# Seven block products for eight from the third feature tile on in the first feed-forward of a two-block model kernel

## What is computed

```python
u = rmsnorm(h, ffn_pre_norm[i])
gate, up = jnp.split(u @ w_gate_up[i], [D_FF], axis=-1)
y = (jax.nn.silu(gate) * up) @ w_down[i]
h = h + rmsnorm(y, ffn_post_norm[i])
```

## Time and profile before

| what | us |
|---|---|
| median of 3 runs | 2981.14 (2980.92 to 2981.69) |
| the profiled execution | 2984.09 |
| its span, first to last instruction | 2982.8 |
| TensorE busy | 2856.0 (96%) |
| VectorE busy | 1855.8 (62%) |
| ScalarE busy | 1205.5 (40%) |
| mean granted TensorE clock | 0.975 of full speed |

### The profile page before, as it was taken

How to read it: one execution, slowest core, us unless ns; L and a number is a source line. 1 busy time by engine, 2 the same in 40 slices (tenths; PEclk the granted TensorE clock), 3 DMA queues, 4 the chain that set the end, 5 groups by cost and what they waited for, 6 DMA issues and landing times.

```text
span 2982.8 us, 36065 instructions
## 1 busy us (share of the span) xinstructions
PE 2856.0 (96%) x14312; PEld 2390.3 (80%) x14312; DVE 1855.8 (62%) x2615; ACT 1205.5 (40%) x1810; POOL 71.3 (2%) x44
## 2 busy tenths in 40 slices
PE   8999989999999999999999977899999999999998
PEld 6878878887788888888778856788887888888887
DVE  4147668625766666667641277577457777777774
ACT  3144446634433323333331166776433333333432
POOL 0002210010000000000000000000000000000000
PEclk9999999999999999999999989887999999999999
DMA  4111130032211111113122100000211111111122
GB/s 170 50 32 46 57 118 19 2 126 78 106 52 50 55 57 50 50 57 127 50 85 64 36 15 10 22 1 1 93 42 43 50 57 57 50 50 57 57 92 85
DMA packets 47831, 172.99 MB, mean 58 GB/s; under 512 B 5648, under 2 KB 6160, under 8 KB 47664
## 3 DMA queue, kind: packets, MB, share of 16 engines
q1 hardware_dynamic: 47664, 170.68, 17.1%
HBM read 145.23 MB, written 25.43 MB: 57 GB/s over the span
## 4 chain that ended last, share of the span: by engine, by line
PE 86%; DVE 8%; ACT 3%; issue 2%; DMA 0%; SPq 0%; DVEq 0%; ACTq 0%
PE PS L295 14%; PE PS L297 14%; PE PS L299 13%; PE PS L1596 8%; PE PS L1597 8%; PE PS L1598 8%; PE PS L483 2%; PE PS L485 2%; PE PS L484 2%; PE PS L1184 2%; PE PS L706 2%; PE PS L3116 1%; PE PS L1154 1%; PE PS L1169 1%; DVE H L2788 1%
## 5 line engine op out<-in xcount | busy, mean ns | idle before, releaser
L1596 PE MATMUL PS<-u_hi_f,w_hi 128*128 128x512 f32 x624 | 242.7, 389 | 0.0
L1597 PE MATMUL PS<-u_lo_f,w_hi 128*128 128x512 f32 x624 | 242.7, 389 | 0.0
L1598 PE MATMUL PS<-u_hi_f,w_lo 128*128 128x512 f32 x624 | 242.7, 389 | 0.0
L289 DVE TENSOR_TENSOR w_lo<-w_raw,w_hi 128x1024 fp32r<-128x1024 f32 x93 | 116.1, 1252 | 202.3 <-ACT w_hi L283 202.3
L1545 ACT ACTIVATE w_hi<-weight_sums 128x512 fp32r<-128x512 f32 x156 | 98.1, 629 | 355.9 <-DVE weight_sums L1566 197.1
L283 ACT ACTIVATE w_hi<-w_raw 128x1024 fp32r<-128x1024 f32 x93 | 97.7, 1055 | 282.2 <-PE PS L299 143.2
L295 PE MATMUL PS<-f_ah,w_hi 128*128 128x512 f32 x640 | 197.1, 389 | 0.1
L297 PE MATMUL PS<-f_al,w_hi 128*128 128x512 f32 x640 | 197.0, 389 | 0.0
L299 PE MATMUL PS<-f_ah,w_lo 128*128 128x512 f32 x640 | 197.0, 389 | 0.0
L1551 DVE TENSOR_TENSOR w_lo<-w_raw,w_hi 128x512 fp32r<-128x512 f32 x205 | 137.2, 687 | 93.0 <-ACT w_hi L1545 93.0
L1596 PE MATMUL PS<-f_T_hi,w_hi 128*128 128x512 f32 x468 | 182.8, 391 | 1.9 <-issue 1.9
(11 more groups left out here) (447 smaller groups left out, 6572.5 us busy)
## 6 DMA issues: line engine op xcount, KB each, us to landing
w_raw<-in_weights SPq DMA_DIRECT2D x215, 512.0 KB, 3.5
H<-in_x_t SPq DMA_DIRECT2D x16, 512.0 KB, 4.2
h_kept<-H SPq DMA_DIRECT2D x16, 512.0 KB, 5.1
H<-h_kept SPq DMA_DIRECT2D x16, 512.0 KB, 6.8
stick_kept<-stick_stage SPq DMA_DIRECT2D x12, 512.0 KB, 2.9
mixer<-stick_kept SPq DMA_DIRECT2D x9, 512.0 KB, 7.2
p_kept<-p_stage SPq DMA_DIRECT2D x8, 512.0 KB, 3.9
p_pp<-p_kept SPq DMA_DIRECT2D x8, 512.0 KB, 8.1
```

The source lines that it names most:

```text
L289: dve.tensor_tensor(self.w_lo[i][:], self.w_raw[i][:], self.w_hi[i][:].bitcast(F32), ALU.subtract).then_inc(*self.s("w_lo").up(g))
L1596: pe.matmul(out, hi[:, self.chunk(k)], rh, start=opens and k == 0, stop=False, skip_group_check=True)
L1597: pe.matmul(out, hi[:, self.chunk(k)], rl, start=False, stop=False, skip_group_check=True)
L1598: mm = pe.matmul(out, lo[:, self.chunk(k)], rh, start=False, stop=k == 3, skip_group_check=True)
```

## The change

FAST_FROM of the first feed-forward goes from 3 to 2 and its skips go. The order of the operand parts on ScalarE and VectorE is rewritten around it: the half-width blocks 0 and 1 (A11, S1) stand before the copy of the rows, blocks 2 and 3 after tile 0; VectorE makes S1 and S2 before the raw operands; T2's low parts follow T1's in tile 0, and T3's stand between tile 1's gate and up. The whole splits of gates[2] and ups[2] are gone.

```diff
--- before.py
+++ after.py
@@ -39,8 +39,8 @@
 WINO = [("A11", "B11", 0), ("S1", "T1", 1), ("S2", "T2", 0), ("A12", "B21", 2), ("S3", "T3", 0), ("S4", "B22", 1),
         ("A22", "T4", 0)]
 WINO_BANKS = [(0, 1, 2), (3, 4, 6)]
-FAST_FROM = (3, 2)
-FAST_SKIPS = ((5, 9, 13), ())
+FAST_FROM = (2, 2)
+FAST_SKIPS = ((), ())
 AHEAD = 4
 
 FILL_HEAD, FILL, FILL_TAIL = 2, [3, 3, 3, 2, 2, 2, 1], [2, 1, 1, 2]
@@ -2043,14 +2043,10 @@
         self.act_statistics_root(tag)
         if n:
             self.act_split(gates[0] + RING)
-        if n:
-            for m in range(2):
-                self.act_ff_block(n, m)
+        for m in range(2):
+            self.act_ff_block(n, m)
         self.act_statistics_rows(tag, self.f_rows[n][:])
         for t in range(FAST_FROM[n]):
-            if n == 0 and t == 2:
-                for m in range(2):
-                    self.act_ff_block(n, m)
             act.wait_ge(*self.dve_freed(self.ff_pairs(t)[0], tag, "gate", t))
             if n == 1:
                 w, at = self.gains, self.gains_at["conv"][0] + 4 * t
@@ -2063,12 +2059,10 @@
             if t == 0:
                 self.act_ff_ah0(n)
             if n == 0 and t == 0:
-                self.act_split(gates[2])
                 self.act_ff_highs(n, ("T2", "T3"))
-            elif n == 0 and t == 1:
-                self.act_split(ups[2])
+            if n == 0 and t == 1:
                 self.act_ff_ah(n, 1)
-            elif t == 0:
+            if t == 0:
                 for m in range(2, 4):
                     self.act_ff_block(n, m)
         self.act_ff_fast(n)
@@ -2107,14 +2101,12 @@
         self.dve_statistics(tag, rows[:])
         if n:
             self.dve_split(gates[0] + RING)
-        if n == 0:
-            for k in range(4):
-                self.dve_ff_raw_operands(n, k)
-        else:
-            for m in range(4):
-                self.dve_ff_sum(n, m)
-            for m in range(2):
-                self.dve_ff_block(n, m)
+        for m in range(4):
+            self.dve_ff_sum(n, m)
+        for m in range(2):
+            self.dve_ff_block(n, m)
+        for k in range(4 if n == 0 else 0):
+            self.dve_ff_raw_operands(n, k)
         dve.wait_ge(*self.act_freed(3, tag, "rows"))
         for t in range(FAST_FROM[n]):
             pg, pu = self.ff_pairs(t)
@@ -2131,10 +2123,8 @@
                     dve.wait_ge(*self.s("f_gated").at(n, t - 1))
                 dve.tensor_tensor(sg[:], self.pair(pg), rows[:], ALU.mult).then_inc(*self.dve_frees(pg, tag, "gate", t))
             if n == 0 and t == 1:
-                self.dve_split(ups[2])
-            if n == 0 and t == 2:
-                for m in range(2):
-                    self.dve_ff_block(n, m)
+                for k in range(4):
+                    self.dve_ff_low(n, "T3", k)
             dve.wait_ge(*self.s("w_used").at(ups[t]))
             if n == 0 and t:
                 dve.wait_ge(*self.s("f_al").at(n, t - 1))
@@ -2145,14 +2135,13 @@
             if n == 0 and t == 0:
                 for i in range(5, KT):
                     dve.wait_ge(*self.d(f"p2_stored{i % 3}").at(i))
-            if n == 0:
-                for k in range(4):
-                    self.dve_ff_low(n, ("T1", "T3", "T2")[t], k)
+            if n == 0 and t == 0:
+                for x in ("T1", "T2"):
+                    for k in range(4):
+                        self.dve_ff_low(n, x, k)
             if t == 0 or n == 0 and t == 1:
                 self.dve_ff_al(n, t)
-            if n == 0 and t == 0:
-                self.dve_split(gates[2])
-            elif t == 0:
+            if t == 0:
                 for m in range(2, 4):
                     self.dve_ff_block(n, m)
                 self.dve_ff_sum(n, 4)
```

## The result

The median went from 2981.14 us to **2989.41 us** (7 runs, 2987.65 to 2992.63): a ratio of 1.0032, with a 95% interval of 1.0023 to 1.0041. 2990.5 us was predicted, in a range of 2987.5 to 2994. The kernel before, run 7 times beside it, spread from 2974.66 to 2983.31 us. The span of the profiled execution went from 2982.8 to 2988.0 us.

What follows compares the result with a forecast made beforehand. TensorE's own stream, 86% of the chain, was taken as the bound, so a later down step passes on whole. 0.5 - 2.7 - 4.6 + 14.2 + 2.0 = +9.4 us, taking the median from 2981.14 to 2990.5 us, range 2987.5 to 2994.

Steps and rivals of the forecast that it cites:

- The path into the wait: Tile 2's head: ups[1] product starts about 766.6 us, raw operands 4.0 us later, second block finished at 783.0 us.
- The rows copy 0.5 us later: ScalarE's copy of the statistics' rows, now behind S1's block, delays TensorE's ups[1] product: 0.5 us more.
- The wait: Before tile 2's third block product, S2 x T2, TensorE waits for ScalarE's copy of the first bank: 14.2 us more.
- The clock: After the new wait in tile 2, TensorE's matmuls run at a lower clock: 2.0 us more.
- What goes: Before tile 2, the old gates[2] split wait and its low clock go, 4.6 us less; fewer matmuls, 2.7 us less.
- The twelve matmuls: Tile 2 goes from 96 to 84 matmuls, twelve fewer at 0.227 us each: 2.7 us less.
- The down step's start: Down projection of tiles 0 and 1 in the first feed-forward begins at 812.8 us, not 803.4.
- Moved loads and skips at nothing: Later loads of units 45 and 46 and the dropped half-buffer skips in the first feed-forward cost nothing.
- B: Wait before tile 2's third block only as small as in the second feed-forward: -3.2 us, 2977.9 us; chance 0.06.
- C: Shorter third-block wait, T2's low parts and copy ready by some 790 us: +2 to +5 us; chance 0.04.
- D: A second wait behind the first, from late VectorE work or unit 45: 3 to 6 us more; chance 0.08.
- Rival A: First bank's copy done by 783 us, so no third-block wait: -6.8 us, 2974.3 us; chance 0.05.

Runs made afterwards that it cites:

- e7: The changed kernel run again without any edit: 2989.1 us, ratio 1.0035 to the kernel before.
- e1: Changed kernel with ScalarE's f_ah of tile 1 moved to step 2 of the fast part and VectorE's f_al to step 3: 2985.7 us, ratio 1.0015.
- e4: Changed kernel with 60 unused matmuls filling the wait between tile 2's second and third block products: 2987.22 us, ratio 1.0019 to the kernel before.
- e8: Kernel before with the whole split of gates[2] moved ahead of tile 0's gating: 2978.9 us, ratio 0.9989 to the kernel before.
- e6: Changed kernel with six skipped half-buffers added, at tiles 3, 5, 7, 9, 11 and 13: 2990.74 us, ratio 1.0039 to the kernel before.
- e2: Changed kernel with only ScalarE's copy of the first block's bank moved earlier, behind halves 2 and 3: 2989.4 us, ratio 1.0027 to the kernel before.
- e3: Changed kernel with both ScalarE's bank copy earlier and f_ah of tile 1 later: 2983.89 us, ratio 1.0007 to the kernel before.
- e5: Changed kernel, same seven products, with ScalarE's and VectorE's head rewritten in the order TensorE needs: 2974.55 us, ratio 0.9978 to the kernel before.

## Why the prediction was right

The prediction worked on the clock of the trace before; the changed run is 0.75 us earlier at the spread (762.22, not 762.97). With that taken off, its steps were:

- *The path into the wait.* Product of ups[1] at 766.6: measured 765.80 + 0.75 = 766.55. The rows copy 0.5 us later: 764.65 + 0.75 - 764.99 = 0.41; this one hangs on when unit 43 lands, and in e7 nothing of it is left. The raw operands 4.0 us later: 765.94 + 0.75 - 762.83 = 3.86. The second block done by 783.0: its last matmul begins at 782.01 + 0.75.
- *The wait.* f_ah of tile 1 near 792.9: 792.75. TensorE resumes at 797.2: 796.99. So 14.2 us was 14.0 by starts (796.24 less 782.01 + 0.23), 13.8 by the profile. e1 shows that it is the order on ScalarE.
- *The clock.* 2.0 us: 1.9 by e4.
- *What goes.* The wait and its clock, 4.6 us: 4.5 by e8. The twelve matmuls, 2.7 us: count and spacing are as expected. From the first to the second block start of tile 2 in the changed kernel twelve matmuls take 779.52 - 776.80 = 2.72 us, 0.227 us each. The Trainium skill, TensorE: Matmul & The Clock Gate, section Back-to-back issue gap, gives about 131 ns; the traces of this kernel don't agree.
- *The down step's start.* 812.8: 811.84 + 0.75 = 812.6. The sum of +9.4 is **+9.2**.
- *Moved loads and skips at nothing.* Unit 45 is issued at 795.5 us and lands 3.5 us later, 799.0; its half-split begins behind the copy of 801.14, without a wait. e6 for the skips.

Rivals B, C and D fall with the rows (13.8 us, and no wait after it). Rival A, the copy in time, did not happen.

Three things in the prediction were less good than its number. First, rival A was priced wrongly: it said that with the copy done by 783 us nothing is waited for, and beside it that the block's own inputs are ready by 786 us. e2 and e3 show the wait that this leaves, 2.5 us, and e3 1.7 us of clock behind it, so in the changed order of VectorE an early copy could not have given -6.8 us. e5 comes out at 0.9978, 6.6 us below the kernel before, but it reorders VectorE too; that this is close to -6.8 is partly luck, as e5 lacks the 0.5 us of the rows and has two gaps of 0.3 us of its own. Second, the edges of the rivals are loose by about half a us (C ends at 2986.1 by its own +5 us, D begins at 2993.5), and the lower end of the range, 2987.5, follows from none of its sums. Third, the median landed 1.1 us from the forecast, while the interval of the ratio is worth about 2.7 us either way: the mechanism is shown by the rows, the closeness of the median is in part luck.

The median rose by 8.3 us, not 9.2, and the one profiled span by 5.2. The profiled run of the changed kernel was 0.75 us ahead at the spread, and later stages account for most of the rest: from the last seven-product block of the first feed-forward to that of the second, the kernel before takes 2840.3 - 1360.6 = 1479.7 us and the changed one 2845.6 - 1368.8 = 1476.8, on the same code, and e7 1478.2 (2843.7 - 1365.5). Of the 2.9 us 1.6 are the clock: behind the wait of 1.9 us in the second feed-forward twelve matmuls take 2272.47 - 2268.06 = 4.41 us in the kernel before. The changed run stays at full clock there, as its rows show:

```profile
2274.91 0.47 PE L1596 MATMUL PS<-f_T_hi,w_hi 128*128 128x512 f32 x1 [1.88 <-issue]
...
2277.75 0.39 PE L1596 MATMUL PS<-u_hi_f,w_hi 128*128 128x512 f32 x1
```

Twelve matmuls take 2.84 us here, with the same wait ahead of them. In the traces of all eleven runs this wait is 1.87 or 1.88 us; ten of them, e7 included, show 4.41 or 4.42 us behind it, and only the first profile of the changed kernel 2.84. So that profile's small span is an exception, and the rest of the 2.9 us isn't located.

## What to carry to other kernels

A block of whole work that is replaced by fewer, finer pieces also loses its cover: before crediting the 12 matmuls, list what stood in program order behind the removed piece on the other engines, and see whether the new pieces need an item near the end of that list. Here 2.7 us of arithmetic were paid with 14 us of waiting and 2 us of clock. The same arithmetic with the list reordered gains 6.5 us in the interval; 4.5 of them are the old wait, which the kernel before could have lost by moving one split (e8). When a wait is broken up, count the clock for each part, as e3 shows, and judge such a change by an interval between two fixed pieces of work around it: it repeated within 0.4 us, whole spans only within several.

## What was not expected

- The same wait of 1.9 us is followed by a low clock in ten traces and not in the eleventh, and after a wait of 13.6 to 13.9 us the next 60 matmuls take 15.60, 15.93 (808.61 - 792.68, e7) or 16.56 us (e6), against 13.72 without the idle time. The cost of an idle time is a spread, here 1.9 to 2.8 us, not one number.
- Two waits of 2.5 and 4.2 us (e3) cost as much, clock included, as one of 9.1 us (e1): intervals 45.26 and 45.60.
- The profile's releaser was wrong or missing for each wait on the copies alone: "issue" for the copy at line 1706 in the changed kernel, VectorE's w_lo in e3, ready 3.9 us earlier. The end of the copy, 0.1 us before TensorE's next matmul, tells it every time.
